# Differential attention on one core: TensorE joins the two softmaxes in all eight heads

## What is computed

```python
HEAD_DIM = 64; N_HEADS = 8; SEQ = 512; Q_BLOCK = 128

s = jnp.einsum('bqhcd,bkhcd->bhcqk', qi, k).astype(jnp.float32) * scale   # c = 0, 1: two score matrices a head
mask = k_pos[None, :] <= pi[:, None]
s = jnp.where(mask, s, -jnp.inf)
p = jax.nn.softmax(s, axis=-1)
a = p[:, :, 0] - lam * p[:, :, 1]
o = jnp.einsum('bhqk,bkhe->bqhe', a.astype(v.dtype), v)

o = rms_norm(o, subln_g[j]) * (1.0 - lam_init)
mix = o.reshape(b, s, V_DIM) @ w_o[j]
```

## Time and profile before

| what | us |
|---|---|
| median of three runs | 2090.12 |
| lowest and highest | 2089.89, 2090.74 |
| the profiled execution's own time | 2086.53 |
| its span, from the first to the last instruction | 2084.7 |
| busy in the span: TensorE | 2033.2 (98%) |
| VectorE | 916.8 (44%) |
| ScalarE | 684.9 (33%) |
| GpSimd | 501.6 (24%) |

### The profile page before, as it was taken

How to read it: one execution, slowest core, us unless ns; L and a number is a source line. 1 busy time by engine, 2 the same in 40 slices (tenths; PEclk the granted TensorE clock), 3 DMA queues, 4 the chain that set the end, 5 groups by cost and what they waited for, 6 DMA issues and landing times.

```text
span 2084.7 us, 39789 instructions
## 1 busy us (share of the span) xinstructions
PE 2033.2 (98%) x16290; PEld 1961.1 (94%) x16290; DVE 916.8 (44%) x1077; ACT 684.9 (33%) x1085; POOL 501.6 (24%) x343
## 2 busy tenths in 40 slices
PE   7999999999799999999999999999988999999997
PEld 7999999988499999999999999999965799999997
DVE  4444333499753333333543333333578543333222
ACT  5222222455452222222233222222266442222221
POOL 1333310133123333210312333300321223333110
PEclk9999999999899999999999999999999999999998
DMA  6333333288323333422553333322676133333321
GB/s 197 91 91 91 102 98 93 76 162 169 72 82 91 91 91 91 116 84 82 147 149 102 91 91 91 113 84 86 180 239 221 41 92 91 91 91 98 110 86 41
DMA packets 357708, 224.15 MB, mean 108 GB/s; under 512 B 8035, under 2 KB 340196, under 8 KB 357484
## 3 DMA queue, kind: packets, MB, share of 16 engines
q1 hardware_dynamic: 339204, 192.29, 31.2%
q0 software_dynamic: 8496, 18.93, 4.7%
q10 hardware_dynamic: 9928, 11.79, 1.9%
HBM read 198.52 MB, written 7.53 MB: 99 GB/s over the span
## 4 chain that ended last, share of the span: by engine, by line
PE 87%; DVE 8%; issue 2%; ACT 1%; DMA 1%; DVEq 0%; ACTq 0%; POOL 0%; SPq 0%; POOLq 0%
PE ps_all L552 84%; DVE conv_b L1321 1%; DVE conv L1321 1%; DVE kprod L1517 1%; DVE s_dec L1523 1%; DVE w_lo L1167 1%; PE ps_all L724 1%; PE ps_all L674 1%; PE ps_all L642 1%; PE ps_all L563 0%; DVE nmx L1453 0%; DMA x<-xT 0%; DVE t_out L1195 0%; PE ps_all L607 0%; DVE t_gate L1195 0%
## 5 line engine op out<-in xcount | busy, mean ns | idle before, releaser
L850 ACT ACTIVATE w_hi<-raw 128x1024 fp32r<-128x1024 f32 (+1 forms) x295 | 333.4, 1130 | 1217.2 <-PE ps_all L552 1202.4
L552 PE MATMUL ps_all<-xg_hi,w_hi 128*128 128x260 f32 x3456 | 700.1, 284 | 11.6 <-DVE xg_lo L1177 9.2
L552 PE MATMUL ps_all<-xg_hi,w_lo 128*128 128x260 f32 x3456 | 697.0, 283 | 0.0
L552 PE MATMUL ps_all<-xg_lo,w_hi 128*128 128x260 f32 x3456 | 696.0, 283 | 0.0
L552 PEld LDWEIGHTS ps_all<-xg_hi,w_hi 128*128 128x128 f32 x3456 | 534.1, 189 | 14.3 <-issue 11.3
L552 PEld LDWEIGHTS ps_all<-xg_hi,w_lo 128*128 128x128 f32 x3456 | 533.5, 189 | 0.0
L552 PEld LDWEIGHTS ps_all<-xg_lo,w_hi 128*128 128x128 f32 x3456 | 532.1, 188 | 0.0
L1167 DVE TENSOR_TENSOR w_lo<-raw,w_hi 128x1024 fp32r<-128x1024 f32 (+1 forms) x295 | 396.3, 1344 | 258.7 <-ACT w_hi L850 258.7
L552 PE MATMUL ps_all<-h_hi,w_hi 128*128 128x260 f32 x1664 | 340.1, 284 | 8.2 <-DVE h_lo L1388 8.0
L552 PE MATMUL ps_all<-h_hi,w_lo 128*128 128x260 f32 x1664 | 338.0, 283 | 0.0
L552 PE MATMUL ps_all<-h_lo,w_hi 128*128 128x260 f32 x1664 | 337.3, 283 | 0.0
(11 more groups left out here) (188 smaller groups left out, 1119.5 us busy)
## 6 DMA issues: line engine op xcount, KB each, us to landing
raw<-w_in SPq DMA_DIRECT2D x175, 512.0 KB, 3.7
raw<-w_out SPq DMA_DIRECT2D x64, 704.0 KB, 4.4
made<-made POOLq DMA_DIRECT2D x41, 256.0 KB, 5.8
raw<-c_in SPq DMA_DIRECT2D x16, 512.0 KB, 4.0
raw<-w_kv SPq DMA_DIRECT2D x16, 512.0 KB, 3.9
page<-cache_k SPq DMA_DIRECT2D x16, 512.0 KB, 4.8
page<-cache_v SPq DMA_DIRECT2D x11, 512.0 KB, 5.3
t_out<-t_gate ACTq DMA_DIRECT2D x64, 65.0 KB, 2.7
```

Of the source, the lines that this page charges most:

```text
L552: mm = nc.tensor.matmul(unit[slot][:, s, :], w[:, c % 2, k * P:(k + 1) * P], m[:, s * HALF:(s + 1) * HALF], start=kk == 0 and i == 0, stop ...
L850: nc.scalar.activation(w_hi[:, c % 2, 0:w], raw[:, c, 0:w], ACT.Copy).then_inc(hi_made, 1)
```

## The change

The number of steps that use the diagonals goes from half of the heads' steps to all of them: from 16 to 32. This is the only line that differs.

```diff
         STEPS = HEADS * (SEQ // P)
-        DIAG_STEPS = HEADS // 2 * (SEQ // P)
+        DIAG_STEPS = 8 * (SEQ // P)
         K_FROM = 2
```

## The result

The changed kernel takes 2096.8 us, the median of six runs (2095.7 to 2098.2), against 2089.6 us for six runs of before next to it: a ratio of 1.004, with a 95% interval of 1.0029 to 1.0051, so 6 to 11 us slower. A second set of five runs, on another occasion, gave 2096.5 against 2088.1 us, 1.0045 (1.0031 to 1.0058). The direction is as forecast. The forecast was 9.4 us; measured are 7.2 and 8.4 us by the medians and 8.4 and 9.4 by the ratios.

What follows compares the result with a forecast made beforehand. TensorE, busy for 98% of the span, was taken as the bound. Added records of 13.5 us, less 1.2 and 0.8 (waits), 0.6 (L713) and 1.6 (clock), gave 9.4 us slower: 2099.5 us, range 2097.8 to 2103.2 us.

Steps and rivals of the forecast that it cites:

- added records: TensorE, heads 4 to 7: ordinary matmuls replace transposes, adding 3.37 us a head, 13.5 us for four heads.
- waits at steps 18 and 22: TensorE's waits for VectorE's sums ahead of these turns, 1.19 and 0.77 us, both go: minus 1.96 us.
- wait ahead of L713: TensorE's wait for VectorE's scaling before the sample weights' turn falls from 1.02 to 0.4 us, giving back 0.6.
- clock in head 5: TensorE's low clock from 1609 to 1613 us, following idle time, no longer occurs: minus 1.57 us.
- ScalarE: Two diagonals in heads 4 to 7 add 0.58 us a step, covered by TensorE's work: zero cost.
- stretch: From the end of step 15's turn to the last output turn's start; the whole forecast was 9.4 us slower.
- The floor of 8.9 us: Least possible loss while TensorE is the bound: 13.5 us less 4.55 us of idle and slow time in heads 4 to 7.
- The clock falling all the same: Rival: TensorE's clock still falls, there or elsewhere; 11.0 us slower, 2101.1 us; chance 0.22.
- ScalarE as the bound: Rival: ScalarE bounds the steps without sample values; up to 2 us more, 2101.5 to 2103 us; chance 0.08.
- VectorE as the pace: Rival: VectorE paces heads 4 to 7, so the kernel gets 2.5 us faster, 2087.6 us; chance 0.04.
- No effect: Rival: the change does not take effect; 2090 us; chance 0.01.
- An ordinary matmul as dear as four transposes: Rival: in heads 4 to 7 it takes four transposes' time, not two; 26.2 us slower, 2116 us; chance 0.02.

Runs made afterwards that it cites:

- the diagonals on VectorE: Changed kernel, but in heads 4 to 7 VectorE instead of ScalarE makes the two diagonals; 2095.6 us, 1.0038 of before.
- four transposes: Kernel before with each transpose of heads 4 to 7 issued four times, VectorE keeping its sums; 2096.2 us, 1.0042 of before.
- 24 steps: Changed kernel with diagonals in heads 4 and 5 too, but not in 6 and 7; 2090.0 us, 1.0011 of before.
- One-pass operands: Changed kernel with exponentials and diagonals in fp32r, so the joining matmuls go in one pass; 2088.0 us, 0.9997 of before.
- ScalarE's pair alone: Kernel before with ScalarE also writing the two diagonals in heads 4 to 7, into an unread tile; 2089.8 us, 1.0009 of before.
- the samples' factor: Kernel before with L1489 as a product with a scalar operand instead of two tensors; 2088.3 us, 0.9999 of before.
- no head with diagonals: Kernel before with the diagonals taken out of heads 0 to 3, which use VectorE's sum too; 2096.7 us, 1.0047 of before.
- steps 0 to 16 and 22: Kernel before with diagonals added in only steps 16 and 22 of heads 4 to 7; 2085.7 us, 0.9987 of before.
- both together: Kernel before with diagonals added in steps 16 and 22, and L1489 given a scalar operand; 2086.1 us, 0.9991 of before.
- filled: Kernel before with step 21's values multiplied and step 22's transposes made three times, in TensorE's idle time; 2086.7 us, 0.9994 of before.
- the second trace of before: Kernel before, unedited, profiled again; 2090.1 us in one run, stretch 57.73 us.

## Why the prediction was right, point by point

| step of the sum | worked out | measured |
|---|---|---|
| added records | 13.5 | 3.38 us a head in heads 6 and 7 (3.37 worked out) |
| waits at steps 18 and 22 | -1.96 | gone, worth -2.3; only about 0.5 of it by taking the sums from VectorE |
| wait ahead of L713 | 1.02 to 0.4 | 1.02 to 0.51 |
| clock in head 5 | -1.57 | -1.6 in the first trace of before, about -3 in two others |
| ScalarE | 0 | 0.3 in the stretch, by the diagonals on VectorE; it lies in the wait ahead of L713 |
| stretch | 9.4 | 8.9 against the first trace, 7.5 against the second |

The rounded terms of the sum as written give 9.3; unrounded they give 9.35 to 9.4.

**The added records.** Right to 0.01 us a head, and shown in three ways: by the changed kernel, by four transposes in each place, and by 24 steps. One-pass operands, which take half of the records away, take the cost away (-9.6 us of stretch).

**VectorE.** The sum of the two waits was right and its reason half so. The prediction listed them as going because the sums go; a kernel with the sums still there loses most of them too. An engine that gets later stops waiting for others. For the total it made no difference, so on this step the number was right for a reason that held in part only.

**The wait ahead of L713.** 0.51 us, within the 0 to 0.8 given. I had expected L1489 to fall to about 0.23 us off GpSimd's work; it met L1725 again and took 0.97, so the later end of the range came. The parts that the prediction names for this path add up to 2.3 to 3.1 us, not to its 2.6 to 3.4; measured are 3.2, from 1609.64 to 1612.81 us, the upper end of the right sum. By the short L1489 that I expected, the same parts leave no wait at all, so that 0.4 came near 0.51 is luck in part.

**The clock.** The direction was right. Of the traces that have before's idle time in step 22 (two of before, ScalarE's pair alone, the samples' factor, no head with diagonals) all five have the fall in head 5 (in the last the granted clock is 0.50 from 1620 to 1622 us); with that idle time taken away or filled, in eight traces (twice the changed kernel, four transposes, VectorE's diagonals, one pass, steps 0 to 16 and 22, both together, 24 steps) and a ninth (filled), none has it. The place of the fall was the same each time, its length was not. The size is the term that was mis-sized: I took the 1.57 us of one trace. By their stretches ScalarE's pair alone paid about as much, the second trace of before and the samples' factor about 3 us, so the mean of the four is 2.3. With 0.7 us more for this term and 0.5 for what follows, 9.4 becomes 8.2, which lies among the measured 7.2 to 9.4; that is an estimate, and what the clock does outside the stretch is not in it. The floor of 8.9 us was no floor, because it was worked out from one execution's fall.

**What was left over.** 0.5 us between 9.4 and 8.9, against the first trace: head 4 costs 1.98 and head 5 0.17 us, where 3.37 - 1.19 = 2.18 and 3.37 - 0.77 - 0.51 - 1.57 = 0.52 follow from the terms. The waits cost more than their brackets say. TensorE in order of time in before, steps 18, 22 and 26:

```profile
1592.59 0.71 PE L674 MATMUL ps_all<-vT,aT 128*128 128x128 f32 x4
...
1604.98 0.71 PE L674 MATMUL ps_all<-vT,aT 128*128 128x128 f32 x4
...
1620.67 0.71 PE L674 MATMUL ps_all<-vT,aT 128*128 128x128 f32 x4
1621.22 0.49 PE L663 MATMUL ps_all<-cst,at_n 128*128 128x128 f32 x3
```

Without a wait, in step 26, the turn starts 0.55 us after these values. With the waits it starts 1.91 us after them in step 18 and 1.48 in step 22, so 1.36 and 0.93 us were lost where the brackets show 1.19 and 0.77: a bracket counts from the end of the last record, and in a dense stream the next one starts about 0.16 us before that end. Another 0.2 us were lost ahead of the values of step 21. The three make up the 0.5 us.

**The rivals.** The clock falling all the same: no, in both traces. ScalarE as the bound: no, by two experiments. VectorE as the pace: no for heads 4 to 7, and yes for much of heads 0 to 3, where taking the diagonals away made TensorE wait 13.9 us for L1467. No effect: the change has its effect. An ordinary matmul as dear as four transposes: no, two, as the rows of heads 0 to 3 had said.

## What to carry to other kernels

Moving work from an engine with room to the one that is the bound costs its full time, so ask it stage by stage: here taking the diagonals away costs 7.3 us in heads 0 to 3, where VectorE is the bound (waits and a lower clock together, from one trace; 9.8 us in the whole program), and adding them costs 3.4 us a head where TensorE is. A wait of the bound engine shows where a little of its time buys more than it costs; two steps more, chosen by their waits, gave 2.7 us, all sixteen lost about 8. Count in what follows a wait: the low clock behind 1.8 us of idle time cost 1.6 to 3 us more.

## What the runs showed of the hardware

- VectorE's product of two tensors on a [64, 1] tile (L1489) takes 0.16 us, or 1.01 (before) and 0.97 (the changed kernel) when it starts inside GpSimd's product of 128x512 and then ends with it. With a scalar operand it took 0.21 us in that place, and the next instruction took 0.90 in place of 0.36. In the one-pass kernel, and in two more, it ran in 0.16 us inside GpSimd's L1736, a power over four elements a row, so not all of GpSimd's work does it. Which operand kinds wait was not tried further.
- A wait of TensorE costs about 0.16 us more than the profile's bracket: 1.36 us for 1.19 and 0.93 for 0.77.
- A joining record of 128 columns takes 0.105 us in fp32r and 0.112 in fp32; the first needs one record a matmul and the second two.
- One kernel's executions differ more than a small change does. Before ran from 2083.4 to 2091.3 us over all occasions. Between its two traces, 2.15 us lie ahead of the end of step 15's turn, where the second shows a granted clock of 0.72 from 1573 to 1584 us, and 1.4 us in the stretch, with the same waits in both. Between the two traces of the changed kernel the stretch agreed to the hundredth. Where the clock does not fall, a stretch between two fixed instructions so shows changes of 0.3 us; where it does, one trace is as rough as the times.
